# Convolution steps of VectorE counted out per pair, and mixer parts ahead of the selection, in a one-core decoder step

## What is computed

```python
def _mixing_sublayer(x, mem_k, mem_v, conv_past, w):
    h = _rmsnorm(x, w['norm_mix_g']) @ w['w_in']
    u_a, v_a, val_b, gate_b, q_m, gl_a, gl_b, gl_m = jnp.split(h, SPLITS, axis=-1)
    y_a, vn = _spatial_gate(gelu(u_a), gelu(v_a), w['a_ws'], w['a_bs'], w['a_ln_g'], w['a_ln_b'])
    glu = val_b * jax.nn.sigmoid(gate_b)
    ext = jnp.concatenate([conv_past, glu], axis=1)
    c = _causal_depthwise(ext, w['b_conv_w'], w['b_conv_b'])      # 31 taps
    y_b = jax.nn.silu(_layernorm(c, w['b_ln_g'], w['b_ln_b']))
    y_m = _mem_attend(q_m, mem_k, mem_v)                          # 4 heads, 256 memory tokens
    merged = (sigmoid(gl_a) * (y_a @ w['w_o_a']) + sigmoid(gl_b) * (y_b @ w['w_o_b'])
              + sigmoid(gl_m) * (y_m @ w['w_o_m']))
    return x + merged @ w['w_out'], vn, ext[:, -(CONV_W - 1):]

def block(xb):                                                    # PEER, all rows
    s = einsum('bhpk,hpnk->bhpn', (xb @ wq).reshape(...), keys)   # 8 heads, two halves, 128 keys
    v1, i1 = top_k(s[:, :, 0], 16); v2, i2 = top_k(s[:, :, 1], 16)
    cv, ci = top_k(v1[..., :, None] + v2[..., None, :], 16)       # of 256 sums
    eid = e1 * N_KEYS + e2                                        # 128 experts for a row
    hid = gelu(einsum('bd,bhkd->bhk', xb, u_tab[eid]))
    return einsum('bhk,bhkd->bd', softmax(cv) * hid, v_tab[eid])
```

## Time and profile before

| what | value |
|---|---|
| median of 3 runs | 2237.01 us (2234.17 to 2238.07) |
| profiled execution | 2238.65 us, span 2236.9 us |
| mean granted TensorE clock | 0.813 |
| bytes moved | 895.56 MB, mean 400 GB/s |
| busy: TensorE, VectorE, ScalarE, GpSimd | 1631.0, 1567.8, 656.0, 721.5 us |
| pairs of portion 0, 1, 2, 3 start at | 295, 764, 1334, 1829 us |

### The profile page before, as it was taken

The page is one execution under the profiler, slowest core; times in us unless marked ns, Lnnn a source line. Parts: engine busy times, 40 slices in busy tenths (PEclk is TensorE's granted clock), DMA queues, the critical chain, the costliest instruction groups (busy, mean ns, idle before and its releaser), DMA issues.

```text
span 2236.9 us, 31355 instructions
## 1 busy us (share of the span) xinstructions
PE 1631.0 (73%) x10944; PEld 1069.0 (48%) x10944; DVE 1567.8 (70%) x4170; ACT 656.0 (29%) x1647; POOL 721.5 (32%) x660
## 2 busy tenths in 40 slices
PE   9999987788797477878788647766999853334334
PEld 9866675566675055554433415543887610000002
DVE  4464269988766667877775577787876686776775
ACT  3121232421414242432132323342223332322222
POOL 0000056332232433342222234531323254454443
PEclk9999998899898588999899757876999865555556
DMA  9699899999899999999999999999999999999997
GB/s 338 250 385 402 335 406 420 384 418 400 327 410 419 422 420 421 422 412 422 421 390 421 421 421 414 409 393 396 420 417 421 409 400 421 422 421 421 422 421 317
DMA packets 127773, 895.56 MB, mean 400 GB/s; under 512 B 16096, under 2 KB 16928, under 8 KB 20480
## 3 DMA queue, kind: packets, MB, share of 16 engines
q0 software_dynamic: 83232, 604.02, 65.6%
q1 hardware_dynamic: 44384, 289.54, 32.1%
HBM read 885.39 MB, written 8.11 MB: 399 GB/s over the span
## 4 chain that ended last, share of the span: by engine, by line
PE 33%; DMA 28%; DVE 24%; issue 4%; ACT 4%; DVEq 3%; POOL 3%; SPq 0%; POOLq 0%; ACTq 0%
DMA uv<-uv_in,idx_u 22%; PE bank L1797 14%; DVE uv L1672 11%; PE bank L2109 5%; PE bank L2453 4%; DMA ring<-w_in 4%; DVE yB L1143 3%; PE bank L1803 3%; POOL uv L611 2%; DMA ring<-cache_in 2%; POOL merged L638 1%; ACT L675 1%; DVEq L1138 1%; ACT diag L1036 1%; DVE x L1695 1%
## 5 line engine op out<-in xcount | busy, mean ns | idle before, releaser
L611 POOL DMA_INDIRECT uv<-uv_in,idx_u x574 | 652.1, 1136 | 1294.5 <-PE bank L2453 634.1
L1672 DVE CUSTOM_DVE_ANT_0 uv<-uv,xrep 128x1024 f32<-128x1024 f32 x576 | 687.4, 1231 | 217.0 <-DMA uv<-uv_in,idx_u 209.6
L2453 PE MATMUL bank<-uv,diag 128*32 128x512 f32 x2176 | 393.0, 803 | 476.2 <-ACT diag L1036 470.3
L1797 PEld LDWEIGHTS bank<-xnT,ring 128*128 128x128 f32 x3168 | 434.5, 202 | 77.4 <-issue 68.3
L1797 PE MATMUL bank<-xnT,ring 128*128 128x160 f32 (+1 forms) x3168 | 456.2, 304 | 1.1 <-DMA ring<-w_in 1.0
L675 ACT ACTIVATE pick<-pick 128x2 f32<-128x2 f32 (+1 forms) x315 | 66.9, 213 | 1053.3 <-DVE pick L1672 1052.5
L2453 PEld LDWEIGHTS bank<-uv,diag 128*32 128x32 f32 x2176 | 49.4, 122 | 663.3 <-ACT diag L1036 598.0
L1143 DVE SCALAR_TENSOR_TENSOR yB<-ext_p,small,yB 128x128 f32<-128x128 f32 x960 | 275.2, 348 | 19.5
L675 ACT ACT_TABLE_LOAD x137 | 175.8, 1283 | 2.4
L1036 ACT ACTIVATE diag<-gated_fold,pick 128x32 f32<-128x32 f32 x574 | 153.1, 314 | 9.8 <-ACT pick L675 0.5
L2109 PE MATMUL bank<-ring,xnT 128*128 128x512 f32 x192 | 88.3, 615 | 0.0
(11 more groups left out here) (323 smaller groups left out, 1848.0 us busy)
## 6 DMA issues: line engine op xcount, KB each, us to landing
ring<-w_in SPq DMA_DIRECT2D x211, 1024.0 KB
uv<-cache_in SPq DMA_DIRECT2D x16, 1024.0 KB, 9.6
ring<-cache_in SPq DMA_DIRECT2D x16, 1024.0 KB
uv<-uv_in,idx_u POOLq DMA_INDIRECT x578, 13.9
uv<-w_in SPq DMA_DIRECT2D x4, 1024.0 KB, 10.3
ring<-w_in SPq DMA_DIRECT2D x6, 512.0 KB, 4.7
ext_s<-state_in SPq DMA_DIRECT2D x2, 1088.0 KB, 14.0
convs_out<-ext_s SPq DMA_DIRECT2D x2, 1088.0 KB, 24.7
```

The lines of the kernel that those rows point to most:

```text
L611: nc.gpsimd.indirect_dma_start(out=uvbuf[2 * b + i], out_offset=None, in_=uv_in, in_offset=bass.IndirectOffsetOnAxis(ap=ids[:, c:c + 1], a ...
L1672: ins = V.tensor_tensor_reduce(out=u, in0=u, in1=xrep[gg % 2][:, :], scale=1.0, scalar=0.0, op0=ALU.mult, op1=ALU.add, accum_out=hid[:, c: ...
L1797: ins = MM(out, w[:, k, P * b:P * (b + 1)], rhs(k), start=k == 0, stop=k == KB - 1)
L2453: ins = MM(vbank[gg % 2][c:c + 32, :], diag[:, t % 4, i], uvbuf[2 * b + i][:, D + 512 * n:D + 512 * (n + 1)], start=first, stop=last)
```

## The change

Only VectorE's program order changes; its instructions are the same.

- The steps of the convolution of odd portions leave the parts of the generator. `TAPS[m][u]` says how many of the 62 must be done by pair u, in proportion to `HEAVY` by k, from the fourth glu's place to two pairs before the sums. `beside_pair[0]` is the function that issues them in the pair, as far as the glus are there. In even portions the steps stay in the generator.
- `pick_pairs` (k=0) and `pick_experts` (k=1) now come behind the mixer's parts and the convolution steps of their pair, in all portions, and `scale_fold(s, 1)` ahead of `pick_experts`. At the other k the selection stays where it was, then come the counted steps, then the mixer's parts; at k=2 and 4 mixer's parts come first.
- In odd portions `norm_c` is cut behind the variance: reciprocal and product come at the place of the gate 14.

Convolution steps per pair with `mixing(1)`, before: at pairs 9 to 33, 4,2,2,2,1,2,3,0,2,0,4,2,2,2,2,2,2,2,4,1,2,2,9,4,4. After: at pairs 4 to 32, 5,3,1,1,1,1,3,3,4,3,1,1,1,1,3,3,4,3,1,1,1,1,3,3,4,3,1,1,1. With `mixing(3)`, before: at pairs 156 to 181, 3,1,2,2,3,3,1,3,5,2,3,6,4,0,3,1,1,1,1,2,1,1,1,0,6,6. After: at pairs 152 to 180, 1,1,3,3,4,3,1,1,1,1,3,3,4,3,1,1,1,1,3,3,4,3,1,1,1,1,3,3,3.

```diff
@@ -226,6 +226,24 @@
 
         return place["glu0"] + (place["sc1"] - place["glu0"]) * (u + 1) / (last + 1)
     return place["sc1"] * (u - LEAD) / (last - LEAD)
+
+
+HEAVY = (1, 1, 3, 3, 4, 3, 1, 1)
+
+
+def taps_by(m):
+
+    us = range(PAIRS * STEPS[(m - 1) % 2])
+    first = next(u for u in us if reach(m, u - 1) >= PLACE[m]["glu4"])
+    last = next(u for u in us if reach(m, u - 1) >= PLACE[m]["csum"]) - 2
+    total, so_far, out = sum(HEAVY[u % PAIRS] for u in range(first, last + 1)), 0, []
+    for u in us:
+        so_far += HEAVY[u % PAIRS] if first <= u <= last else 0
+        out.append(-(-2 * CONV_W * so_far // total))
+    return out
+
+
+TAPS = {m: taps_by(m) for m in range(1, PORTIONS, 2)}
 
 
 def stepper(work):
@@ -1150,7 +1168,7 @@
                     dve.wait_ge(taps_made, KB * l + c + 1)
                     V.tensor_reduce(yB[:, c, P:P + T_S], taps_s[:, :, :, :].rearrange("p n t w -> p (n t) w"), AX.X, ALU.add).then_inc(taps_summed, 1)
 
-                done = [0]
+                done, glued = [0], [0]
 
                 def conv(n):
 
@@ -1158,6 +1176,14 @@
                         if done[0] < 2 * CONV_W:
                             convolve(4 * (done[0] // CONV_W), (done[0] % CONV_W,))
                             done[0] += 1
+
+                def conv_upto(n):
+
+                    while done[0] < n and glued[0] >= 4 * (done[0] // CONV_W + 1):
+                        conv(1)
+
+                if p:
+                    beside_pair[0] = conv_upto
 
                 yield place["rows"]
                 if m != 1:
@@ -1204,6 +1230,7 @@
                     if m == 0 and c == 2:
                         dve.wait_ge(S["memsq"], 1)
                         V.tensor_reduce(rb_mem, kT.rearrange("p c t -> p t c"), AX.X, ALU.add).then_inc(S["memred"], 1)
+                    glued[0] = c + 1
                     if p == 0 and c == (4 if m == 0 else 2):
                         dve.wait_ge(S["pe_memsq"], at("pe_memsq", m, 1))
                         V.tensor_scalar(rb_mem, s_bank[0][:, 0:M], 1.0 / D, EPS, ALU.mult, ALU.add).then_inc(S["memvar"], 1)
@@ -1244,7 +1271,8 @@
 
                 def beside(name, taps):
                     yield place[name]
-                    conv(taps)
+                    if p == 0:
+                        conv(taps)
 
                 def max_sample(j):
                     dve.wait_ge(S["pe_sk"], at("pe_sk", m, 4 * j + 4))
@@ -1325,8 +1353,6 @@
                         yield from beside("pts0", 1)
                         max_sample(1)
                     yield place["va3"]
-                    if m == 1:
-                        conv(2)
                 for t in range(1 + p):
                     r = ROWS[t]
                     dve.wait_ge(S["va"], at("va", m, 4))
@@ -1349,11 +1375,10 @@
                     for n in range(6, 8):
                         yield from beside(f"sv{n}", 1)
 
-                def gated(first, last, taps):
+                def gated(first, last):
                     for c in range(first, last):
 
                         yield place[f"mg{c + 1}"] + 2 if c % 8 == 0 else place[f"mg{c}"]
-                        conv(taps)
                         dve.wait_ge(S["pe_proj"], at("pe_proj", m, c + 1))
                         dve.wait_ge(S["gsig"], at("gsig", m, c + 1))
                         gate_c, out = sg[:, c % 2, 0:nt], merged[:, c % KB, 0:nt]
@@ -1424,7 +1449,7 @@
                         if i == 1:
                             yield from beside("ua3", 1 if m == 3 else 2)
                         yield place[f"sg{i}"]
-                        conv((2, 1, 2, 0)[m])
+                        conv((2, 0, 2, 0)[m])
                         if m == 0 and i == 3:
                             conv(2 * CONV_W)
                             dve.drain()
@@ -1452,6 +1477,8 @@
                     yield place["csq"]
                     dve.wait_ge(S["pe_csq"], at("pe_csq", m, 1))
                     V.tensor_scalar(rb[:, 0:nt], t_bank[:, 0:nt], 1.0 / D, EPS, ALU.mult, ALU.add).then_inc(S["cvar"], 1)
+                    if p:
+                        yield place["mg14"]
                     dve.wait_ge(S["rt_c"], at("rt_c", m, 1))
                     V.reciprocal(rb[:, 0:nt], rb[:, 0:nt])
                     dve.drain()
@@ -1476,19 +1503,18 @@
                     yield from gated_rows(4, 0)
                     yield from gated_rows(5, 0)
                 else:
-                    taps = 1 if m in CACHED else 2
-                    yield from gated(0, 3, taps)
+                    yield from gated(0, 3)
                     yield from norm_v_gain()
-                    yield from gated(3, 5, taps)
+                    yield from gated(3, 5)
                     yield from norm_v_bias()
-                    yield from gated(5, 8, taps)
+                    yield from gated(5, 8)
                     yield from spatial()
-                    yield from gated(8, 12, 3 if m in CACHED else 4)
+                    yield from gated(8, 12)
                     conv(2 * CONV_W)
                     yield from centre()
-                    yield from gated(12, 14, 0)
+                    yield from gated(12, 14)
                     yield from norm_c()
-                    yield from gated(14, 24, 0)
+                    yield from gated(14, 24)
 
                 for i in range(4):
                     yield place[f"out{i}"]
@@ -1735,6 +1761,7 @@
             def layer(s):
                 return next(i for i in range(PORTIONS) if s < FIRST[i + 1]) // 2
 
+            beside_pair = [None]
             V.memset(one, 1.0).then_inc(one_set, 1)
             V.memset(yB[:, 0, 0:P], 1.0).then_inc(ones_set, 1)
             dve.wait_ge(consts_landed, 16)
@@ -1754,11 +1781,7 @@
                     if t == 0:
                         pick_half(1, 0)
                         pick_half(1, 1)
-                    if k == 0 and s + 1 < NSTEP:
-                        pick_pairs(s + 1)
-                    elif k == 1 and s + 1 < NSTEP:
-                        pick_experts(s + 1, layer(s + 1))
-                    elif k == 3 and s + 1 < NSTEP:
+                    if k == 3 and s + 1 < NSTEP:
                         gates(s + 1)
                     elif k == 5 and s + 1 < NSTEP:
                         scale_fold(s + 1, 0)
@@ -1772,8 +1795,14 @@
                         scale_fold(s, 1)
                     if k == 2 and s % 2 == 0 and s:
                         add_group(s // 2 - 1)
+                    if m % 2 == 0:
+                        beside_pair[0](TAPS[m + 1][u])
                     if mix:
                         mix(reach(m + 1, u - 1))
+                    if k == 0 and s + 1 < NSTEP:
+                        pick_pairs(s + 1)
+                    elif k == 1 and s + 1 < NSTEP:
+                        pick_experts(s + 1, layer(s + 1))
                     if m == PORTIONS - 1 and u == 20:
                         final(0, slice(0, P), 0)
                     if m == PORTIONS - 1 and u == 24:
```

## The result

| | before | after |
|---|---|---|
| median of 5 runs | 2235.87 us (2234.17 to 2238.07) | 2273.91 us (2270.69 to 2275.71) |
| profiled execution, span | 2238.65, 2236.9 us | 2273.91, 2272.2 us |

The ratio is 1.0167, with a 95% interval from 1.0152 to 1.0181: the change costs 38 us, where 19 were forecast. The time lies inside the range (2226 to 2274) by 0.1 us.

What follows compares the result with a forecast made beforehand. VectorE was taken to set the pace from pair 4 to 33 (busy 217.4 of 246 us); portions 0, 1 and 2 cost 13 + 1 + 5 = +19 on 2237, so 2256 us, range 2226 to 2274 (its own 2243 to 2272).

Steps and rivals of the forecast that it cites:

- portion 0: Portion with mixing 1: losses 16.5 less gains 3.7, taken as +13 us; bounds -10 and +19.
- Rival B: Levelling works: hump at pairs 31 to 33 gone, transfers recover, half of 18.8 us won; 2228 us, chance 0.26.
- rival C: VectorE's lateness falls within what the transfer queue holds and is made good; 2237 us, 4 either side, chance 0.12.
- rival D: Steps at pairs 4 to 8 lengthen beside GpSimd's products, +4.3 us and the products as much; 2265 us, chance 0.07.
- The rule of the Trainium skill: Interleaving stretches bound by different engines can gain; by it the levelled steps would bring 10.4 us back.
- 8, glu and tap sum: Pair 8: with pick_pairs later, only some 3.0 us of work fills the 4.8 us before the tap sum: +1.8.
- 10, exponent sum: Pair 10: VectorE reaches L1241 at 377.2, before the exponent sum's read-out at 379.97; +2.6 us taken.
- 31 to 33, gates: Pairs 31 to 33: without eight covering steps VectorE waits for TensorE; +3 us for two gates, bounds 0 and 9.4.
- 36 and 37, norm: Split norm: the reciprocal's 3.27 us wait for the root goes, the swish comes some 2 us later: -1.3.
- portion 2's term: Mixing 3: same +13 us less 8 that the queue swallows, as TensorE waits 29.0 for transfers: +5, bounds -8 and +15.
- theory C: Cover theory, stated with the experiments: VectorE is full, and each wait that selection or steps covered before is now paid.

Runs made afterwards that it cites:

- experiments 4: Changed kernel with the old numbers of steps per pair, still counted out behind the dots: 2274.46 us, 1.0172 of before.
- experiment 7: Kernel of before with mixing 1's hump lowered inside the mixer: 3 steps a gate for the first eight gates, 2 for gates 8 to 11; 2235.62 us, 0.9995.
- Experiment 6: Kernel of before with the norm in two parts and 12 steps put earlier, ahead of tap sums where VectorE waits for GpSimd: 2235.80 us, 1.0005 of before.

## Why the prediction was right, and where it was not

**The direction and portion 0 held.** VectorE sets the pace up to pair 34, its work stays as it was, and the loss is idle time; +13 was forecast and 13.9 measured. Rival B is refuted by experiments 4 and 7, rival C (nothing comes of it) by the result, and rival D's sum by VectorE's busy time (215.80 and 215.59 us). The groups of VectorE from 320 to 583 us show the same:

```profile
L1698 DVE CUSTOM_DVE_ANT_0 uv<-uv,xrep 128x1024 f32<-128x1024 f32 x61 | 74.1, 1251 | 0.0
L1161 DVE SCALAR_TENSOR_TENSOR yB<-ext_p,small,yB 128x128 f32<-128x128 f32 x240 | 70.2, 354 | 5.2 <-issue 0.2
```
They are as long as in the earlier trace rows. But D's mechanism is in the trace. The first four step instructions of pair 4, and GpSimd's product beside them:

```profile
329.52 2.25 DVE L1159 TENSOR_SCALAR yB<-ext_p,small 128x128 f32<-128x128 f32 x4
330.29 2.72 POOL L656 TENSOR_TENSOR merged<-ext_s,small 128x248 f32<-128x248 f32 x4
```
Before, at pair 9 and with no product beside them, they took half:

```profile
369.00 1.12 DVE L1141 TENSOR_SCALAR yB<-ext_p,small 128x128 f32<-128x128 f32 x4
```
With four more at pair 8 (2.06 us instead of 1.14) the steps of portion 0 are some 3 us longer, of D's 4.3. It adds nothing to the sum, since fewer dots and selection instructions now run beside a product. The rule of the Trainium skill that was weighed against the sum (Perfetto Trace Analysis, Optimization Strategy) did not help: evening out gave nothing by itself (0.9995 in experiment 7, and 1.0172 against 1.0167 with and without the old numbers).

**The terms of portion 0**, by what each pair lasts longer than before, less 1.17 us for each step that it has more:

| pair | forecast | changed kernel |
|---|---|---|
| 4, steps beside the product | 0 | +2.1 |
| 5, tap sum | -1.2 | -2.1 |
| 8, glu and tap sum | +1.8 | +3.9 |
| 10, exponent sum | +2.6 | +0.2 |
| 17, v part | +3.1 | +1.9 |
| 24 and 25, gates | +1.8 | +4.1 |
| 31 to 33, gates | +3 | +9.6 |
| 34, last steps | -1.2 | -1.3 |
| 36 and 37, norm | -1.3 | -4.1 |
| 40 and 41, gates | +4.2 | +3.0 |
| 46 and 47 | 0 | -3.9 |

The pairs not listed add up to +0.5, with -1.6 at pair 9, -2.1 over 18 to 23 and +2.2 over 52 to 58 as the largest. The sum of portion 0 came out at +13 by errors that cancel, and that is luck. Between these places no pair adds more than 0.9 us while the lead goes from 8 to 16 steps: taking steps early costs nothing by itself, as the prediction said. The waits at 31 to 33 were under-sized: they reach the upper bound of 9.4 us. "For two gates" ignored that the gate needs TensorE's products of the spatial sum just ahead of it (32 matmuls, 4.5 us in the changed kernel and 6.6 in 4, the first gate needing a part of them) and the sigmoid.

At pair 10 the row was read wrongly. VectorE's timeline after:

```profile
388.49 0.15 DVE L1263 TENSOR_SCALAR stat<-stat 128x1 f32<-128x1 f32 x1
388.56 0.15 DVE L1268 RECIPROCAL stat<-stat 128x1 f32<-128x1 f32 x1
```
ScalarE's:

```profile
391.21 0.20 ACT L693 ACTIVATION_READ_ACCUMULATOR merged<-bank,stat 128x1 f32 x1
```
The reciprocal runs 2.7 us ahead of that read-out and waits for nothing: it belongs to the head before. The read-out at 379.77 in the earlier trace rows was the next head's. The trace of before says so too: the reciprocal ran ahead of that read-out.

```profile
379.57 0.15 DVE L1241 RECIPROCAL stat<-stat 128x1 f32<-128x1 f32 x1
```

**The step that failed is portion 2's term**, "part of VectorE's lateness is no lateness": +5, and 20.6 measured. TensorE's waits for weights and cached rows after, from 1375 to 1792 us, beside the earlier trace rows:

```profile
PE bank L2004 <- DMA ring<-cache_in: 11.3, 3, 8.8
PE bank L2029 <- DMA ring<-cache_in: 8.1, 3, 4.4
```
They fell from 29.0 to 19.4 us. The wait for the next weights, which the prediction left out, fell as well. Before and after:

```profile
PE bank L1803 <- DMA ring<-w_in: 5.8, 1, 5.8
PE bank L1826 <- DMA ring<-w_in: 1.4, 1, 1.4
```
With another of 1.0 us before, TensorE's waits for transfers fell by 15.0 us, where 8 was put down for what the queue swallows. So that size was low, but on the side that makes the change cheaper. What made the term too small is the gross price taken over from portion 0. This portion has waits of its own: pair 152 (the selection no longer ahead of the tap sum, +4.8), the exponent sums at 161 and 164 (+6.4), the gates at 170 (+8.5), the spatial sum at 177 (+4.5), pairs 180 and 181 (+5.9), and the gates and output parts at 184 to 192 (+8.1). These are 38 us gross, where 13 was taken, and some 18 come back, most at 165 (-5.8) and 178 (-3.7).

**The range.** 38 us is twice the +19, and 2273.91 lies 0.1 us inside the upper bound of 2274. The prediction's own 2272 needs the upper bounds of portions 0 and 2 together (19 + 1 + 15 = 35), not one of them as it says; only with both is the range wide enough. That the time fell inside it is luck.

**What replaces theory C.** Neither cover alone nor load alone decides. From pair 4 to 34 VectorE had 27 us to spare in 243, 14 of them in waits for other engines and 5 in the short gaps of the steps; a new wait then costs nearly its length. With 34 us less work to do, the new order's longer waits cost 12 us instead of 17 there, and 5 us instead of 14 in pairs 152 to 182. Experiment 6 fits this: in portion 2 the old order stands at a bound other than VectorE (half the steps shorten pairs 152 to 208 only from 444.5 to 442.5 us), so delay is paid and haste is not. Which bound this is, TensorE's ordered queue or the order of its weight loads, was not measured, and so it is argued and not shown that delay passes through it. Nor is it settled why the counted numbers cost 7 us with the selection in front and none behind it; runs of that kernel differ among themselves by 10 us.

## What to carry to other kernels

Independent work is worth most between a result that an engine gives away and the answer that it waits for. Moving it a few instructions to the other side of the wait costs the wait, even if every engine does the same work in the same pair; count what stands in the gap, not what stands in the stretch. Where two kinds of work cover the same wait, removing either may cost nothing and removing both the whole wait (pair 32: 0.0, 0.1 and 2.6 us), so edits measured one by one don't add up (24 us apart, 38 together). A wait for GpSimd is a poor place for work that GpSimd slows down. Price a term from the rows of its own stretch, also when the code is the same as in another.

## What was not expected of the hardware

A step beside GpSimd's tap products takes about twice as long. After, four instructions at pair 153 took 2.26 us instead of 1.14, and four at pair 4 took 2.25 instead of 1.12. Twelve at pair 5 took 3.56, as elsewhere: no product ran beside them. Before, no step instruction overlapped a product. In the changed kernel 20 of 992 do, with a mean of 0.69 us against 0.35. Over the stretch from 320 to 583 us this hardly shows in the mean (354 ns against 352), because so few are met; in experiment 6, which puts steps there by intent, it does (368 against 347).
